# Mean squares of the background norms: float32 squares summed on GpSimd, one matmul with ones for each tile

## What is computed

```python
def rmsnorm(x, g):
    xf = x.astype(jnp.float32)
    r = lax.rsqrt(jnp.mean(xf * xf, axis=-1, keepdims=True) + RMS_EPS)
    return (xf * r).astype(x.dtype) * g
...
x = macaron_half_ffn(x, *ffn1)                    # x + 0.5 * (silu(h wg) * (h wu)) wd, h = rmsnorm(x)
q, k, v, u = split_projection(rmsnorm(x, mix_norm), w_in)
x = x + concat([attention(q, k, v), s5(u)]) @ w_out
x = macaron_half_ffn(x, *ffn2)
y = rmsnorm(x, final_norm)
```

## Time and profile before

| | us |
|---|---|
| three runs | 1339.89, 1455.2, 1494.41 (median 1455.2) |
| the profiled execution | 1338.18 |
| its span on the slowest core | 1336.6 (the cores lie between 1319.4 and 1336.6) |
| PE busy | 1241.2 |
| DVE busy | 667.6 |
| ACT busy | 393.2 |
| POOL busy | 126.9 |

### The profile page before, as it was taken

One profiled execution on the slowest core, in us unless ns is written; L12 is line 12 of the kernel. 1 busy time (PEld: TensorE's weight loads), 2 busy tenths in 40 slices (PEclk: granted clock), 3 DMA queues, 4 the chain that ended last, 5 costly groups with the idle time before them and its releaser, 6 DMA issues.

```text
span 1336.6 us, 21400 instructions; the slowest of 8 cores (1319.4 to 1336.6 us)
## 1 busy us (share of the span) xinstructions
PE 1241.2 (93%) x7695; PEld 666.2 (50%) x7774; DVE 667.6 (50%) x1357; ACT 393.2 (29%) x686; POOL 126.9 (9%) x210
## 2 busy tenths in 40 slices
PE   4698899998999999999989899999999979999997
PEld 1243344444566446665546544334445545666665
DVE  2355765354178537844362266568834543232226
ACT  2343411533212432223342213432234431101123
POOL 2011120011000000000120000000010000110000
PEclk9898999999999999999999999999999989999999
DMA  9356644358244324434492243334455249464323
GB/s 216 63 115 185 147 84 80 60 78 103 37 103 79 60 41 93 86 65 66 62 126 37 58 90 65 59 76 86 83 82 95 33 105 193 74 115 80 64 33 135
DMA packets 62263, 117.35 MB, mean 88 GB/s; under 512 B 24072, under 2 KB 30632, under 8 KB 61872
## 3 DMA queue, kind: packets, MB, share of 16 engines
q0 software_dynamic: 43632, 80.79, 38.2%
q1 hardware_dynamic: 18528, 35.18, 8.5%
HBM read 183.39 MB, written 15.37 MB: 149 GB/s over the span
## 4 chain that ended last, share of the span: by engine, by line
PE 77%; DVE 8%; DMA 5%; issue 4%; ACT 3%; SPq 1%; DVEq 0%; ACTq 0%; POOLq 0%
PE ps L205 69%; PE psy L205 9%; DMA wf<-wgu 3%; ACT rt_s L209 2%; SPq L83 1%; DVE hA_s L215 1%; DMA scr_tab<-hB_s 1%; ACT L209 1%; DVE hA_s L212 1%; DVE xT_s L215 1%; DVE mix_s L212 1%; DVE hB_s L212 1%; DVE aT_s L212 1%; ACT sg_s L209 1%; DMA xT_s<-xT 1%
## 5 line engine op out<-in xcount | busy, mean ns | idle before, releaser
L205 PE MATMUL ps<-hB_s,wf 128*128 128x384 bf16 (+1 forms) x2112 | 334.8, 320 | 11.5 <-DVE aT_s L212 4.7
L205 PE MATMUL ps<-hA_s,wf 128*128 128x512 bf16 x1370 | 320.6, 392 | 26.3 <-DMA wf<-wgu 9.8
L205 PE MATMUL ps<-aT_s,wf 128*128 128x512 bf16 (+4 forms) x1611 | 303.5, 343 | 10.5 <-DVE xT_s L215 6.4
L209 ACT ACTIVATE sg_s<-ps 128x512 f32<-128x512 f32 (+3 forms) x284 | 147.8, 537 | 548.5 <-PE ps L205 468.6
L212 DVE TENSOR_TENSOR aT_s<-ps,sg_s 128x512 bf16<-128x512 f32 (+2 forms) x220 | 129.9, 595 | 336.6 <-PE ps L205 243.9
L205 PEld LDWEIGHTS ps<-hB_s,wf 128*128 128x128 bf16 x2112 | 207.2, 99 | 136.1 <-issue 20.1
L205 PEld LDWEIGHTS ps<-hA_s,wf 128*128 128x128 bf16 x1408 | 139.7, 100 | 201.5 <-issue 51.3
L205 PEld LDWEIGHTS ps<-aT_s,wf 128*128 128x128 bf16 x1628 | 154.8, 98 | 152.7 <-issue 28.7
L215 DVE SCALAR_TENSOR_TENSOR xT_s<-ps,xT_s 128x384 f32<-128x384 f32 (+4 forms) x188 | 108.1, 576 | 177.7 <-PE ps L205 177.1
L83 POOL DMA_DIRECT2D wf<-wgu x88 | 47.2, 537 | 688.5 <-PE ps L205 653.1
L209 ACT ACT_TABLE_LOAD x37 | 47.5, 1283 | 91.3 <-PE ps L205 59.6
(11 more groups left out here) (177 smaller groups left out, 836.4 us busy)
## 6 DMA issues: line engine op xcount, KB each, us to landing
wf<-wgu POOLq DMA_DIRECT2D x88, 512.0 KB, 5.4
wf<-wd POOLq DMA_DIRECT2D x59, 352.0 KB, 4.4
scr_tab<-hB_s SPq DMA_DIRECT2D x8, 512.0 KB, 6.8
hA_s<-scr_tab SPq DMA_DIRECT2D x16, 256.0 KB, 3.8
hB_s<-scr_tab SPq DMA_DIRECT2D x16, 256.0 KB, 4.1
yT<-xT_s SPq DMA_DIRECT2D x8, 512.0 KB, 7.5
xT_s<-xT SPq DMA_DIRECT2D x4, 768.0 KB, 5.8
wm_s<-wout POOLq DMA_DIRECT2D x12, 256.0 KB, 3.7
```

Source lines behind the costliest of these rows:

```text
L205: return self.P.op('pe', lambda e: e.matmul(out, lhsT, rhs, start=start, stop=stop, skip_group_check=skip), waits=waits, signal=signal)
L209: return self.P.op('act', lambda e: e.activation(out=out, in_=in_, func=func, **kw), waits=waits)
```

## The change

The squares of a background norm are written in float32 and added up on POOL over the eight chunks, and one matmul with ones for each tile takes the sum. `square_sum` takes the place of `square` in `norm_first_b`, in the second down part of `ffn` and in `mix_tail`; `norm_fin` sees by `tok_add` which of the two a tile has had. `norm_now` and `down_last` are left as they were.

```diff
@@ new, behind square
+    def square_sum(self, kc, ti):
+        hf = 0 if ti < 2 else 1
+        t0, n = TT[ti]
+        l0 = (t0 - HBASE[hf]) // 2
+        f = self.hf[hf].bitcast(F32).rearrange("p (k t) -> p k t", k=KC)
+        row = lambda k: f[:, k:k + 2, l0:l0 + n // 2]
+        two = lambda ap: ap.rearrange("p (a t) -> p a t", a=2)
+        dst = row(0) if kc == 0 else row(2 + 2 * (kc % 2))
+        t = self.act(dst, two(self.xs(kc, ti)), AF.Square,
+                     waits=[self.tok_x[(kc, ti)]] + self.h_free[hf] + ([self.tok_add[(kc - 2, ti)]] if kc > 2 else []))
+        if kc == 0:
+            self.tok_add[(0, ti)] = t
+            return
+        out = two(self.hs(6, ti)) if kc == KC - 1 else row(0)
+        self.tok_add[(kc, ti)] = self.tt(out, row(0), dst, ALU.add, waits=[t, self.tok_add[(kc - 1, ti)]], eng='pool')
+
+    def norm_sum(self, ti, bank):
+        n = TT[ti][1]
+        return self.mm(self.ps[bank][:, :n], self.ones[:], self.hs(6, ti), True, True,
+                       waits=[self.tok_add.pop((KC - 1, ti)), self.t_const] + self.psr[bank], signal=True)
@@ norm_fin
-        for kc in range(KC):
+        summed = (KC - 1, ti) in self.tok_add
+        if summed:
+            t_mm = self.norm_sum(ti, bank)
+        for kc in range(0 if summed else KC):
@@ norm_first_b
-                self.square(kc, ti)
+                self.square_sum(kc, ti)
@@ ffn (twice) and mix_tail (twice)
-                        self.square(*a)
+                        self.square_sum(*a)
```

More of the change, by code:

```diff
@@ L325, in alloc @@
         self.mring = Ring(P, "wmd", [self.wm[:, 0:1024], self.wm[:, 1024:2048]])
-        self.tok_x, self.tok_h, self.tok_sq = {}, {}, {}
+        self.tok_x, self.tok_h, self.tok_sq, self.tok_add = {}, {}, {}, {}
         self.tok_q, self.tok_k, self.tok_v, self.tok_u, self.tok_y = {}, {}, {}, {}, {}
```

## The result

The changed kernel takes 1348.41 us (median of 8 runs), the kernel before 1337.63 on the same chip: ratio 1.0083 [1.0070, 1.0096], some 11 us slower. Forecast were 1340.0 us and no change that could be told. In some executions of either kernel the cores of one die show a lower granted clock and take longer (here one of 1419.1 us, with 0.90 to 0.92 on cores 0 to 3), and the ratios compare executions without that.

What follows compares the result with a forecast made beforehand. PE, busy 1241.2 of 1336.6 us, was taken as the bound, with 18.7 us of its work going; +7 - 2.5 - 2.3 - 1.5 + 1.6 + 0 = +2.3 us on 1338.2 gave 1340, range 1325 to 1354.

Steps and rivals of the forecast that it cites:

- A: First norm of tiles 2 to 4 (247 to 285 us): POOL's adds pace ACT, PE waits for an evacuation; +7 us.
- C: Input projection of tiles 2 to 4 (683 us): PE earlier to the group ahead of its wait; -2.3 us.
- D: Second norm of tiles 0 and 1 (668 us): PE 3.0 us earlier, final adds can hold DVE; -1.5 us.
- B: Input projection of tiles 0 and 1 (305 us): ACT's table load, which waits for PE, comes forward; -2.5 us.
- E: Second norm of tiles 2 to 4 (1023 to 1061 us): wout load issued late behind an add; +1.6 us.
- F: Final norm of tiles 0 and 1 (1067 and 1095 us): savings fall into waits for DVE and weights; 0 us.
- Rival 1: All places: the adds are hidden everywhere, being as short as the squares; 1326 us, chance 0.20.
- Rival 2: POOL becomes the bound of both bursts, adds taking twice the row's work (decides from about 1.7); 1376 us, chance 0.05.
- Rival 3: First norm of tiles 2 to 4: eight DVE holds reach PE rather than one, 7.4 us added; 1348 us, chance 0.13.

Runs made afterwards that it cites:

- gain alone: Kernel before with no adds, bf16 squares and one ones-matmul a tile, the mean leaving out seven of eight chunks: ratio to before 0.9946.
- cost alone: Changed kernel with its adds, but eight ones-matmuls on each tile's sum, so PE saves nothing: 1352.82 us, ratio to the kernel before 1.0125.
- C alone: Against the kernel before, sums only in the second down part of ffn 1 half 1: ratio 1.0001.
- wout ahead: Changed kernel with the last output projection's squares two groups behind instead of one; two runs, no ratio, first-to-last stretch there 74.0 us (changed kernel 75.9).
- A undone: Changed kernel with `norm_first_b` back to bf16 squares and eight ones-matmuls, the other four places keeping sums: 1336.01 us, ratio to the kernel before 0.9990.
- D and E: Against the kernel before, sums only in the output projections of half 0 and half 1, the latter's squares two groups behind: ratio 0.9972.
- tile 2 of A: Added to D and E: the sum for tile 2 alone in `norm_first_b`; 1331.44 us, ratio to the kernel before 0.9951 (second run).

## Why the forecast was wrong

The time fell into the range and the shape of A was foretold, but the sum of +2.3 us was 10 us short, and with it the claim that nothing could be told. By its steps:

- **A (+7, measured +11.1): right mechanism, terms too small.** From PE's first down group (core 0: 255.53 before, 248.24 after) Exp ended 9.6 us later, not 8.4, because an add with its hand-over took 1.14 us and not 1.04. That is two errors that in part cancel, by luck: the add alone takes 1.00 us, not the 0.83 of the line through the int32 rows, and the hand-over 0.14, not 0.21, which I read from a row whose wait DVE ended, not POOL. The one hold of 1.0 us was right (3.21 for 2.20). PE's group began 8.0 us later; I had 5.6 + 1.0 = 6.6. The clock took 2.1 us (9.41 against 7.29), not 1.4: my row was one after an idle of 4.5 us, here it was 10. And two further waits (0.59 and 0.93) came from more holds, where I had counted only the first. Together 8.0 + 2.1 + 1.5 - 0.95 = 10.7 of the 11.1.
- **C (-2.3, measured +3.0): the step that failed.** It failed twice. "14 x 0.16 = 2.3 us earlier to the group whose Silu and multiplies stand ahead of PE's wait" took the ones-matmuls for pure load; they covered a Silu (with no adds at all PE waits 1.26 us for it), and gain alone gives 0.1. And the final adds were charged to D, as a loss of part of its gain; they hold the multiplies of D's norm, but after D's first gate matmul, so D kept its 2.6 us and C paid 2.4 to 2.7 (cost alone, C alone).
- **B (-2.5, measured -1.2):** the same cover. PE's second gate group began 1.09 us late, for the Silu, and then 32 matmuls took 6.07 us for 5.36. Gain alone has the same two numbers, so the adds are not in it.
- **D (-1.5, measured -2.6):** inside its range, near the end with the larger gain; see C.
- **E (+1.6, measured +1.0):** right, and a little less. Up to the last `wout` matmul E is 1.2 us longer (medians), and with the loads ahead of the adds 0.65 us shorter than before (wout ahead), within what the waits for `wout` differ between cores. The ones-matmuls, which I gave nothing, return 0.15.
- **F (0, measured +1.0):** in the other kernels it moves between 19.0 and 21.5; I did not settle it.

Rival 1 falls with the adds' length. Rival 2 falls too: an add took 1.2 times the row's work, not 1.7, and that POOL sets the pace at A was the forecast's own view. That float32 squares cost ACT nothing held (mean 479 ns for the hB tiles, 478 before). Rival 3 was half right. The holds did spread: DVE's norm multiplies are 6.2 us longer for the hB tiles alone (43.6 for 37.4). By the rule of the Trainium skill (SBUF — State Buffer, section "SBUF: two separate sides"), whichever of a GpSimd operation and a VectorE operation with two SBUF inputs starts first has the pair for the whole instruction and the other blocks; the trace agrees: an add of 1.26 us at 267.80 fell beside four multiplies, and they took 1.01 us longer (3.21 for 2.20). But of what they cost DVE only 1.74 us reached PE at A when A's own chain was out of the way (A undone), and 2.4 to 2.7 at C.

## What to carry over

Work that one engine does while another prepares its next input is not all saving: before removing it, look which wait it covers, and give the gain only down to that wait. And when work moves to a slow engine, compare its length with the gap at each place separately: here the same edit is worth -2.6 us where two down groups cover the relay and the adds are spread out, and +11 where 21 adds stand in one burst ahead of a table load. An engine that also issues the weight loads should have them ahead of such work, not behind (here 1.8 us at E, between the changed kernel and wout ahead).

## What was not expected of the hardware

A float32 add on POOL took 1.29 us on average for 512 columns, 1.01 for 384 and 0.87 for 320, about a fifth more than an int32 multiply of 512 (1.05) and the line through it; in bf16 it was little shorter, 0.91 for 1.00 us with 384 columns and no DVE multiply beside it. At F, D and E with and without tile 2 of A have 19.0 us on most cores for 20.3, in rows of PE where the waits are the same or shorter but the clock was low one group earlier (core 0 of D and E: 7.04 us at 0.75 for the first 32 gate matmuls, 5.34 at 1.00 for the 30 after PE's wait for `aT_s`; before 5.36 at 1.00 and 6.62 at 0.76). Wout ahead, with the same order at E, has 20.6. Whether it can be had on purpose was not tried.
